# Two transformer blocks on one core: waits of TensorE at six seams made finer or put later

## The reference

```
first_block:   h = rms_norm(x);  q_d, k_d, v_d, u_p, q_m, gates = split(h @ w_in)
               mix = gate0 * (diff_attention @ w) + gate1 * (pool @ w) + gate2 * (memory_attention @ w)
               x = x + rms_norm(mix @ w_out)
               up = causal_conv3(rms_norm(x) @ w_up);  g, v = split(up)
               x = x + rms_norm((gelu(g) * v) @ w_down)                     # 2816 hidden features
second_block:  for i in (0, 1):
                 sh, sc, g = split3(silu(cond) @ mod_w[i] + mod_b[i])       # for x and for the context
                 h, hc = rms_norm(x) * (1 + sc) + sh, rms_norm(ctx) * (1 + sc_c) + sh_c
   i = 0 even:   y = concat(attention_A * silu(ag), attention_B * silu(bg)) @ ev_w_out   # x and ctx
   i = 1 odd:    oc = silu(layer_norm(conv31(cv * sigmoid(cgl)))) * silu(cg)
                 y = concat(oc, neighbourhood_attention(dq, dk, dv) * silu(dg)) @ od_w_out
                 x = x + g * y   (and ctx after i = 0)
               return rms_norm(x) * final_g
```

## Time and profile before

| | us |
|---|---|
| median of 3 runs | 1881.06 |
| lowest and highest of them | 1874.99, 1881.57 |
| the profiled execution's own time | 1877.81 |
| its span, first to last instruction | 1876.4 |
| mean granted clock of TensorE | 0.967 |
| TensorE busy, 9464 matmuls | 1754.5 (94%) |
| VectorE busy | 1016.8 (54%) |
| ScalarE busy | 747.3 (40%) |
| GpSimd busy | 588.3 (31%) |

### The profile page before, as it was taken

One profiled execution on the slowest core, in us unless ns is written; L12 is line 12 of the kernel. 1 busy time (PEld: TensorE's weight loads), 2 busy tenths in 40 slices (PEclk: granted clock), 3 DMA queues, 4 the chain that ended last, 5 costly groups with the idle time before them and its releaser, 6 DMA issues.

```text
span 1876.4 us, 24708 instructions
## 1 busy us (share of the span) xinstructions
PE 1754.5 (94%) x9464; PEld 1401.0 (75%) x9464; DVE 1016.8 (54%) x2024; ACT 747.3 (40%) x1460; POOL 588.3 (31%) x257
## 2 busy tenths in 40 slices
PE   7999999899999899999999899999899978999987
PEld 5889666778888688887887677655568867896666
DVE  2798454532242533434787524666643577975543
ACT  5222345533233444444223341466643134225532
POOL 3776222243344144444443021100003223521131
PEclk9999999999999799999999799999999989999999
DMA  7555221132234133332753021100001432221021
GB/s 226 168 167 159 67 63 57 57 101 73 74 90 135 34 90 101 92 99 88 213 153 108 12 75 45 34 1 1 2 12 57 136 92 84 79 68 46 23 79 45
DMA packets 255363, 155.25 MB, mean 83 GB/s; under 512 B 5969, under 2 KB 250894, under 8 KB 255246
## 3 DMA queue, kind: packets, MB, share of 16 engines
q1 hardware_dynamic: 251998, 147.12, 26.7%
q10 hardware_dynamic: 3248, 6.55, 1.1%
HBM read 151.55 MB, written 2.10 MB: 82 GB/s over the span
## 4 chain that ended last, share of the span: by engine, by line
PE 83%; DVE 7%; ACT 4%; issue 4%; DMA 1%; POOL 1%; ACTq 0%; SPq 0%; DVEq 0%; POOLq 0%
PE ps L747 65%; PE ps L2167 3%; PE ps L2178 2%; PE ps L2197 2%; PE ps L960 1%; PE ps L1509 1%; PE ps L1493 1%; PE ps L1457 1%; DVE probs L2269 1%; PE ps L1015 1%; DVE h_lo L1050 1%; PE ps L1501 1%; ACT w_hi L687 1%; DVE scaled_hx L1057 1%; PE ps L2203 0%
## 5 line engine op out<-in xcount | busy, mean ns | idle before, releaser
L728 POOL TENSOR_TENSOR w_lo<-w_raw,w_hi 128x1024 fp32r<-128x1024 f32 (+1 forms) x220 | 547.6, 2493 | 1222.6 <-ACT w_hi L687 1222.4
L747 PE MATMUL ps<-h_hi,w_lo 128*128 128x512 f32 x1088 | 439.3, 404 | 21.5 <-DVE h_lo L1050 8.3
L747 PE MATMUL ps<-h_hi,w_hi 128*128 128x512 f32 x1088 | 428.3, 394 | 0.0
L747 PE MATMUL ps<-h_lo,w_hi 128*128 128x512 f32 x1088 | 428.2, 394 | 0.0
L747 PEld LDWEIGHTS ps<-h_hi,w_lo 128*128 128x128 f32 x1088 | 207.1, 190 | 82.7 <-issue 19.1
L687 ACT ACTIVATE w_hi<-w_raw 128x1024 fp32r<-128x1024 f32 (+1 forms) x220 | 228.6, 1044 | 43.0 <-PE ps L747 35.8
L747 PEld LDWEIGHTS ps<-h_hi,w_hi 128*128 128x128 f32 x1088 | 206.8, 190 | 44.6
L747 PEld LDWEIGHTS ps<-h_lo,w_hi 128*128 128x128 f32 x1088 | 207.7, 191 | 41.4 <-issue 1.4
L1442 DVE SCALAR_TENSOR_TENSOR mod_sums<-mod_raw,small,mod_sums 128x256 f32<-128x256 f32 x252 | 150.8, 671 | 0.0
L2252 ACT ACTIVATE probs<-probs,small 128x512 f32<-128x512 f32 (+3 forms) x128 | 93.7, 733 | 24.0 <-DVE small L2269 21.4
L1887 DVE SCALAR_TENSOR_TENSOR conv<-ps,cols,conv 128x511 f32<-128x511 f32 x44 | 33.0, 750 | 125.4 <-ACT conv L1850 125.4
(11 more groups left out here) (410 smaller groups left out, 3277.1 us busy)
## 6 DMA issues: line engine op xcount, KB each, us to landing
w_raw<-in_w_in SPq DMA_DIRECT2D x56, 512.0 KB, 5.3
mod_raw<-in_mod_w SPq DMA_DIRECT2D x24, 1024.0 KB, 5.4
w_raw<-in_w_up SPq DMA_DIRECT2D x44, 512.0 KB, 3.8
w_raw<-in_od_w_in SPq DMA_DIRECT2D x28, 512.0 KB, 3.8
w_raw<-in_ev_w_in SPq DMA_DIRECT2D x20, 512.0 KB, 3.8
w_raw<-in_w_down SPq DMA_DIRECT2D x16, 512.0 KB, 3.9
w_raw<-in_w_mem_kv SPq DMA_DIRECT2D x8, 512.0 KB, 3.9
w_raw<-in_w_attn_branch SPq DMA_DIRECT2D x8, 512.0 KB, 4.0
```

Source lines behind the costliest of these rows:

```text
L728: POOL.tensor_tensor(wlo[:, p, 0:n], raw[:, p, 0:n], f(whi[:, p, 0:n]), ALU.subtract).then_inc(*chunk_lo.by(c))
L747: ins = PE.matmul(out, l, r, start=first and n == 0, stop=last and n == 2)
```

## The change

At each seam a wait is split, moved behind other work, or given another bank:

- the down product's first tile waits for `ffn_lo(kf)` at each of its 22 features;
- the late modulation is multiplied behind tiles 1, 3, 5, 7 of `wo2`; its banks 3 and 7 are exchanged; the sum for hx1 waits for chunk 10 and `u0` for chunk 11;
- the spread of the context's norm c1 stands behind the first tile of `u1`;
- `act_squares` has no table load of its own and `act_rms` can leave out both of its loads; the load for the root stands before the evictions of `wo`, `dn`, `wo2` and `wo3`;
- `wo2` waits for `g_prod("bg", 2)` instead of 3;
- `cg` has the banks 1, 2, 3, 0; its first three tiles are issued before the wait, which is for `g_prod("dg", 2)`;
- `wo3` takes the features in the order 4, 5, 6, 7, 0, 1, 2, 3 and waits for each in its first tile.

```diff
@@ -592,7 +592,7 @@
...
     for name, n in (("u0", 4), ("u1", 4), ("dq", 4), ("dk", 4), ("dv", 12), ("cg", 4), ("wo3", 8)):
-        in_ring(name, n, by_table(name), dict(dk=TWO, dv=(1, 3)).get(name, (0, 1, 2, 3)))
+        in_ring(name, n, by_table(name), dict(dk=TWO, dv=(1, 3), cg=(1, 2, 3, 0)).get(name, (0, 1, 2, 3)))
 
@@ -749,30 +749,30 @@
...
 
-    def pe_tile(job, u, xs, hi, lo, kt, ready=None):
+    def pe_tile(job, u, xs, hi, lo, kt, ready=None, order=None):
 
...
         for n, (xh, xl, tok_) in enumerate(xs):
-            for k in range(kt):
+            for i, k in enumerate(order or range(kt)):
                 if ready:
...
                 ins = mm3(bank(b + (1 if job == "vB" else 4) * n, tok_), hi[:, k], lo[:, k], xh[:, k, 0:tok_], xl[:, k, 0:tok_],
-                          k == 0, k == kt - 1)
-                if k == 3 and kt == 8 and tok_ == SEQ and n == 0:
+                          i == 0, i == kt - 1)
+                if i == 3 and kt == 8 and tok_ == SEQ and n == 0:
                     yield
...
 
-    def pe_gemm(job, xs, ready=None, after_tile=None):
+    def pe_gemm(job, xs, ready=None, after_tile=None, order=None):
 
...
             hi, lo = chunk_views(c)
-            for _ in pe_tile(job, u, xs, hi, lo, DT, ready if u == 0 else None):
+            for _ in pe_tile(job, u, xs, hi, lo, DT, ready if u == 0 else None, order):
                 yield
@@ -946,7 +946,6 @@
...
 
-        ACTE.preload_act_table(ACT.Sqrt)
         for t in range(DT):
@@ -988,14 +987,15 @@
...
 
-    def act_rms(name, preload=True):
+    def act_rms(name, preload=True, then=ACT.Exp):
         nb = tokens(name) // P
...
                         bias=eps).then_inc(*rms.by(name))
-        ACTE.preload_act_table(ACT.Exp)
+        if then:
+            ACTE.preload_act_table(then)
 
@@ -1446,7 +1446,7 @@
...
     def mod_bank(layer, m):
-        return (3, 7)[m % 2] if layer == 1 and m >= MOD_LATE else 4 + m % 2
+        return (7, 3)[m % 2] if layer == 1 and m >= MOD_LATE else 4 + m % 2
 
@@ -1797,8 +1797,9 @@
...
 
+        ACTE.preload_act_table(ACT.Sqrt)
         run(act_take("wo", evict))
-        act_rms("mix")
+        act_rms("mix", False, None)
         act_squares("h2", xT, lambda t: ACTE.wait_ge(*x_added("mix", t)))
@@ -1820,7 +1821,6 @@
...
         run(pe_gemm("up", X, ready=lambda n, k: PE.wait_ge(*n_lo("h2", k))))
-        PE.wait_ge(*ffn_lo(FT - 1))
         for c in range(24):
@@ -1829,6 +1829,8 @@
...
                 kf = 8 * kk + k
+                if u == 0:
+                    PE.wait_ge(*ffn_lo(kf))
                 ins = mm3(bank(ring_bank("dn", u)), hi[:, k, :], lo[:, k, :], fhi[:, kf, :], flo[:, kf, :], kf == 0,
@@ -1875,7 +1877,7 @@
...
         run(act_take("dn", evict_down))
-        act_rms("ffn")
+        act_rms("ffn", False, None)
 
@@ -2488,7 +2490,7 @@
...
 
-    LATE_WEIGHED, LATE_PRODUCT = {0: 0, 1: 2, 2: 4, 3: 6}, {2: 0, 4: 1, 6: 2, 7: 3}
+    LATE_WEIGHED, LATE_PRODUCT = {0: 0, 1: 2, 2: 4, 3: 6}, {1: 0, 3: 1, 5: 2, 7: 3}
 
@@ -2498,7 +2500,7 @@
...
         pe_gated("bg", XC)
-        PE.wait_ge(*g_prod("bg", 3))
+        PE.wait_ge(*g_prod("bg", 2))
         run(pe_gemm("wo2", [(Tail(ghi, CTX), Tail(glo, CTX), SEQ), (Tail(ghi, 0), Tail(glo, 0), CTX)],
@@ -2525,13 +2528,17 @@
...
     def pe_odd_projections():
-        PE.wait_ge(*mod_set(1, MOD_CHUNKS - 1))
+        PE.wait_ge(*mod_set(1, MOD_CHUNKS - 2))
         pe_sum_of_sum("hx1", acc["layer"], summed("layer", DT - 1))
         pe_spread("hx1", 5)
+        PE.wait_ge(*mod_set(1, MOD_CHUNKS - 1))
         run(pe_gemm("u0", X, ready=lambda n, k: PE.wait_ge(*n_lo("hx1", k))))
         pe_sum_of_sum("c1", wdiag["c1"], summed("c1", DT - 1))
+        u1 = pe_gemm("u1", X)
+        next(u1)
+        next(u1)
         pe_spread("c1", 5)
-        run(pe_gemm("u1", X))
+        run(u1)
         run(pe_gemm("dq", X))
@@ -2579,7 +2586,7 @@
...
         act_load_bias(1)
-        act_rms("hx1")
+        act_rms("hx1", False)
         act_apply("hx1", hhi, shift(1, 0))
@@ -2765,14 +2772,16 @@
...
         pe_gated("dg", X, {1: pe_ln_spread})
-        PE.wait_ge(*g_prod("dg", 3))
-        run(pe_gemm("cg", X))
+        cg = pe_gemm("cg", X)
+        for _ in range(6):
+            next(cg)
+        PE.wait_ge(*g_prod("dg", 2))
+        run(cg)
 
         def ready(n, k):
-            if k < 4:
-                PE.wait_ge(*g_lo("cg", k))
-
-        run(pe_gemm("wo3", [(ohi, olo, SEQ)], ready=ready))
+            PE.wait_ge(*(g_lo("cg", k) if k < 4 else g_lo("dg", k - 4)))
+
+        run(pe_gemm("wo3", [(ohi, olo, SEQ)], ready=ready, order=(4, 5, 6, 7, 0, 1, 2, 3)))
 
@@ -2825,7 +2835,7 @@
...
     def act_end():
-        act_rms("final")
+        act_rms("final", False, None)
         ACTE.wait_ge(*tile_done("wo3", 7))
```

## The result

The kernel after takes 1857.7 us, median of 4 runs (1854.5 to 1860.0), beside 1879.9 for the kernel before (median of 4 too). The ratio is 0.9883, interval 0.9865 to 0.9900: faster by 22 us. Predicted were 1857, and 1850 to 1867.

What follows compares the result with a forecast made beforehand. TensorE was taken as the bound, busy for 94% of the span with 83% of the chain. Terms -0.8 + 1.3 + 4.3 + 1.6 + 7.9 + 7.0 = 21.3 off 1877.8 gave 1856.5; predicted 1857, range 1850 to 1867.

Steps and rivals of the forecast that it cites:

- A: Down product by feature: weighing ends at 907.7, TensorE waits 5.8 us before the modulation's product; gain -0.8 (bounds +3.4, -3.1).
- with none: At the down product: the weighing ends at 905.9 if no POOL operation falls inside it; 907.7 was taken.
- tempting: At the down product: 4.6 + 1.9 = 6.5 us, won only without the modulation's product in TensorE's queue.
- B: Summary norms: the 1.28 us table load before hx0's squares goes; gain 1.3, and 0 at mix, ffn and the end.
- C: Gate banks, even layer: the 3.01 us wait before wo2 and its half clock go; gain 4.3, bounds 2.8 and 4.6.
- D: Late modulation at wo2's end: 2.6 us instead of 4.5 from last tile to sum; gain 1.6, bounds 0 and 2.5.
- E: u1's first tile before the context norm's spread: idle 4.58 us and half clock go; gain 7.9, bounds 3 and 8.2.
- Rival 1: VectorE's convolution becomes the bound, its 7.62 us of room used up by E; 5.4 lost, 1862; chance 0.12.
- F: Odd layer's cg and wo3: 5.59 us idle and half clock before cg go; gain 7.0, bounds 4.5 and 7.6.
- Sum: All six seams together gain 21.3 us: 1856.5 from the profiled execution, 1859.8 from the median; predicted 1857.
- Rivals 2 to 4: Late weight chunks in E or F, 1862 (0.13); half clock stays, 1863 (0.08); late products outrun VectorE, 1878 and above (0.02).

Runs made afterwards that it cites:

- second profile: Kernel after run once more, unchanged, for a second profile: 1857.6 us, ratio to before 0.9872.
- product moved: Kernel after with the modulation's product of chunk 0 moved behind the first third of the second down tile: 1851.9 us, ratio to before 0.9854.
- E alone: Kernel before with only u1's first tile put before the spread of c1: 1868.2 us, ratio to before 0.9951.
- F alone: Kernel before with only cg's first three tiles before the wait, cg's banks and wo3's feature order changed: 1869.5 us, ratio to before 0.9955.
- A alone: Kernel before with only the down product's first tile waiting for each f_lo: 1875.7 us, ratio to before 0.9987.
- B alone: Kernel before with only the square-root table loads moved or dropped: 1880.0 us, ratio to before 0.9989.

## Why the prediction was right

- **A** failed in sizes, not in mechanism. The wait came before the product and the half clock behind it. But the weighing ended at 906.86, on the clock of before (1.1 less) 905.8, and not 907.7: the GpSimd operation behind the eviction did begin inside it, but VectorE went on and GpSimd waited. So the weighing took 5.62, the end that was priced "with none". So TensorE waited 3.3, not 5.8. The half clock cost 0.8 in the product (1.58 against 0.81 from start to start) and 2.5 in the second tile (17.7 against 15.2), 3.3 in all. The prediction's text says 1.9 and its sum takes 2.2, without saying why. The product stood 3.5 sooner than before: 3.5 - 3.3 = 0.2. Two errors of opposite sign, and so luck. In the second profile, with a wait of 2.88 and the shorter half clock, it is 2.0. The "tempting" 6.5 is near what the moved product then gave, 5.7 and 6.8.
- **B** was sized at 1.3 and came at 1.4 alone, at 2.1 and 1.7 in after. At ffn the root came sooner and VectorE's diagonal took 1.65 for 1.27, ending at the same distance: 0, as priced.
- **C** is right, 4.5 for 4.3, by the profile of before, which had the half clock behind the wait. E alone and F alone have the same wait of 3.01 and full clock, and stand 1.7 better there without the edit; against those C is worth its lower bound, 2.8. First before, then E alone:

```profile
1456.60:1459.40 2.80, 2.80 (x8) 2.21 (x7) 2.34 (x3) 1.32 (x2) 1.40 (x1) 0.50 1.15 326
```

```profile
1456.60:1459.40 2.80, 2.80 (x14) 2.28 (x13) 2.45 (x3) 1.21 (x2) 1.52 (x1) 1.00 1.16 327
```

- **D**: 1.4 for 1.6. From the product behind the last tile to the sum 2.9 us, for 2.6.
- **E**: 7.4 for 7.9. No chunk was late and no half clock came. One step was wrong and harmless: VectorE's first wait was not used up, since the convolution ended 2.7 us sooner, counted from a matmul ahead of the seam: u1's tiles, its inputs, are sooner too. 7.6 - 7.4 + 2.7 = 2.9, the wait seen. Rival 1 had less for it than it was given.
- **F**: 7.5 for 7.0; the bank wait of 1.84 lies in its 1.4 to 2.6 and takes the place of 1.82. Where the half clock comes behind it the seam gives 5.9 (second profile, product moved). The prediction tied the half level to waits of 3 us and more. That was too narrow already for the trace of before, which has a stretch at 0.50 (401.6 to 408.4) behind a wait of 1.08 (at 401.25).
- **Sum**: in the first profile the seams gave 23.1 and the other stages took 5.3 back, which makes 17.8; in the second 22.9 and 2.8, which makes 20.1. Most of the 5.3 are stretches at half clock, which differ between two executions of one program. The medians differ by 22.2. So the seams were summed 1.6 to 1.8 too low, the stages set at nothing went the other way, and that the median lies within 1 us of 1857 is luck: the timing can't tell 3. Rivals 2 to 4 did not occur: no chunk was waited for in E or F, the clock was full where the waits of C, E and F are gone, and no wait stood before a late product.

The prediction takes VectorE for the loser each time that it meets GpSimd. For the multiplications that is so. One in before with GpSimd idle, then one in after with the GpSimd operation that it meets:

```profile
1807.14 1.09 DVE L2803 SCALAR_TENSOR_TENSOR pg<-sg,conv_y 128x512 f32<-128x512 f32 x1
```

```profile
1788.66 2.40 POOL L728 TENSOR_TENSOR w_lo<-w_raw,w_hi 128x1024 fp32r<-128x1024 f32 x1 [2.64 <-ACT w_hi L687]
1789.82 2.19 DVE L2813 SCALAR_TENSOR_TENSOR pg<-sg,conv_y 128x512 f32<-128x512 f32 x1
```

GpSimd had begun 1.2 us sooner, and VectorE's operation ends 0.95 after GpSimd's. At seam A it is GpSimd that begins second and stands still. The Trainium skill (SBUF — State Buffer, section "SBUF: two separate sides") gives the shared pair of ports to whichever starts first, for the whole instruction, and has the other one fully blocked. The multiplications agree. At seam A the loser is the one that the page names, but it stands still for 1.3 to 2.5 us, over several of VectorE's operations of 0.47; and in before GpSimd's operation, begun behind the first of the row, went in between two of them. The prediction's choice of VectorE cost 1.9 us of A, 907.7 for 905.8.

## What to carry to other kernels

Before a wait is split, read what stands next in the same engine's queue: if that hangs on the same event, as the product here did by way of a load, the wait only moves behind the tile, and the half clock with it; move both. A seam's worth is better read as a shift between the same instructions in two traces than from a time: terms of 1 to 8 us were told apart so, where the timing resolves 3. Read the shift in two profiles all the same, since the half clock alone moved two seams by 1.4 to 1.6 us. When a wait is removed, count the wait as sure and the half clock behind it as possible: behind the wait of 3.01 it came in three of five profiles.

## What the hardware showed that was not expected

- The half clock behind a wait is not settled by the program. The wait of 3.01 before `wo2` had it in the profiles of before, A alone and B alone, and not in those of E alone and F alone. The wait of 1.8 before `wo3` had it in three of ten profiles (the second of after, product moved, E alone), and cost 1.6 us more there. Two profiles of after differ in stretches of unchanged code, and the stages outside the seams took back 5.3 us in one and 2.8 in the other.
- Where the half clock came behind nearly the same wait (2.88 and 3.32), it lasted 3.4 us in one execution and 6.8 in another. With the 0.44 of the wait this makes the 1.8 us between the two at seam A.
- Of VectorE and GpSimd either can be the one that stands still, and at seam A it goes by the program. In all five profiles without edit A the weighing gives way: one of its operations takes 2.6 to 2.7 us and the 14 take 7.8. In all seven with it the weighing keeps its 5.62, and GpSimd's operation of 768 columns takes 3.2 to 4.3 us instead of 1.86 and ends 1.7 us behind VectorE's row of weighing and addition, whenever it began. So it seems to have waited for the end of the whole row. What decides who gives way stays open: the rows fit both the size of GpSimd's operation and the moment at which it begins.
